# Joined attention: item order, split output products, key copies ahead of the exponential, and two moves at the end of the feed-forward stage

## The chip, the cores and the metric

The kernel runs on one core of one Trainium2 chip. The metric is the device time of one execution in microseconds (us), as a median over executions. "The profile" is one execution taken by the hardware profiler; its times are from the start of its span. Engines: PE is TensorE (PEld its weight loads), DVE is VectorE, ACT is ScalarE, POOL is GpSimd, SP is SyncE, which here only issues DMAs.

## The reference, cut to what matters

One decoder layer over a prompt (16 meta tokens and 1024 prompt tokens) and 8 sample sequences of 4 tokens with 2048 cached positions each:

```python
a = rmsnorm(hp, g_mix)
q_r, k_r, v_r, g_r, q_lat, q_pe, c_kv, k_pe = mixer_inputs(a, ...)   # one input projection
o_r, st = retention_prompt(q_r, k_r, v_r, log_gamma)
o_lat = mla_prompt(q_lat, q_pe, c_kv, k_pe)      # causal softmax, 4 heads, blocks of 128 queries
hp = hp + mixer_output(o_r, g_r, o_lat, w_uv, w_out)
hp = hp + conv_ffn(rmsnorm(hp, g_ffn), ...)      # up-projection, width-3 conv, silu gate, down-projection
# the sample rows do the same, with mla_attend over the paged cache (page_table) and their own tokens:
s = (einsum('bqhc,bkc->bhqk', q_lat, c_kv) + einsum('bqhr,bkr->bhqk', q_pe, k_pe)) * SOFTMAX_SCALE
p = softmax(where(mask, s, -inf)); out = einsum('bhqk,bkc->bqhc', p, c_kv)
```

After the final rmsnorm the outputs are y for prompt and samples, the new latents and rope keys, the retention states and the last convolution rows.

## The kernel before, in words

The stages follow one another: input projection (until about 330 us), retention and latent projections, the joined attention (442 to 695 us), output projection, feed-forward up-projection with convolution and gate (22 steps), down-projection (77 steps), final norm. Each product of two float32 operands of the large projections is three passes of split operands (high by high, high by low, low by high), so that PE is the busy engine.

**Attention** (`attention`, from L1180) interleaves two jobs. The prompt job has 36 *items* (`items`, L1184), one per pair of a query block j (0 to 8) and a head h (0 to 3). Item j covers 16 queries for j = 0 and 128 for the others, and its keys are 16 + 128 j columns, in `nb = j + 1` blocks. The sample job walks 32 cache *pages* (each page number of four sequences at once), one in each of the iterations k = 0 to 31. The last four iterations, k = 32 to 35, have no page. Pages form groups of four, called *probability blocks* B; at k = 4B+4 the scores of block B are reduced and exponentiated (`block_max` on DVE, `block_exp` on ACT), at k = 4B+5 its probabilities are turned and weighed against the latents (`fill probs`, `weigh`).

PE's program, iteration k, in this order: the scores of item k+1 (`score_part`); two fills that turn the page's latent keys (`keys` 0 and 1); the value products of item k-1 (`value_part`); a third fill that turns the page's rope keys (`keys` 2); the fills of block B (`probs`, `own`) if there is one; the fills that turn item k's probabilities, four blocks of 128 keys per fill (`turn`); the page's scores (`page_scores`); a `self` fill in k = 15 and 31; `weigh`; `close` and `head_values` for the end of a group of sequences.

A *fill* is a run of transposes into one of two PSUM banks of a ring (`ring_b`, fill n uses bank n % 2). PE may start fill n only when fill n-2 has been copied out (`wait_left`). Which engine copies is fixed: ACT takes `keys` 0 and 2 and the first and third `turn`; DVE takes `keys` 1, the second `turn`, `probs`, `own`, `self` and `close`. `page_scores` waits for all three keys copies, and in the first page of a block (k % 4 = 0) for `block_exp` of the block before, since that frees the bank of the page scores.

ACT's program, iteration k: copy `keys` 0; exponential of item k+1 (`exp_part`); `block_exp` if k % 4 = 0; copy `keys` 2; copies of the turns; the output of item k-1 to its high part (`hi_part`). DVE's: `block_max`; `take_part`; masking and row maximum of item k+1 (`max_part`); copy `keys` 1; `probs`, `own`, `block_sum`; the second turn; `close`; the low part of item k-1's output (`lo_part`, after `hi_part`); `self`; scaling of item k+1's probabilities (`scale_part`). `value_part(k)` waits for all turn copies of item k and for `lo_part(k-1)`; `weigh` waits for `lo_part(k-1)`.

Pages are loaded by SP and POOL, eight buffers deep. The four buffers of block B come free in `weigh(B)`. When the last page is weighed, SP also loads the first half of the output weights (`room.load_out`).

**The end of the feed-forward up-projection** (step n = NF-1 = 21). ACT: `second_out` twice, `split_d(0..3)` (high parts of the first four down-projection steps, two copies each, four buffers), `tap2` of the a half (waits for DVE's `add_first`), `first_out` of the g half (takes product 4 of the last step out of PSUM), `tap2` of the g half, `split_d(4)`, `silu`. DVE: `lo_a`, `lo_w` of steps 0 to 3, then `add_first`, the taps, steps 4 and on. PE: the down-projection. Its step 0 has four tiles of three products; tiles 2 and 3 write the banks that `first_out` must have emptied (`pe.wait_ge(S["ug1"], NF - 1 if m < 2 else NF)`). After steps 4 to 9 PE turns the convolution states (`state_turn`); when ACT has copied them all (`st_out`), SP stores them and then issues the loads of step 15 and on (`load_lanes`).

## Time and profile before

| | us |
|---|---|
| median of 3 runs | 1544.28 (1540.99 to 1544.93) |
| the profiled execution's own time | 1536.31 |
| its span | 1534.6 |
| PE busy | 1463.2 (95%) |
| DVE busy | 803.4 (52%) |
| ACT busy | 588.1 (38%) |
| POOL busy | 389.4 (25%) |

A row of the timeline gives start, length, engine, source line, operation, output <- inputs, shapes (stationary and moving operand for PE), a count of merged instructions, and in brackets how long the engine had been idle before it and what ended the idleness. PE instructions overlap, so that the distance between two starts tells the pace better than a length. PEclk is the clock granted to TensorE as a share of full speed: 1.00 is 2.4 GHz, 0.50 is 1.2 GHz.

### The profile page before, as it was taken

The numbers are of one execution on the slowest core, as the hardware profiler recorded it, in microseconds if no ns is written. First come the engines' busy times: TensorE is split into PE (matmuls) and PEld (weight loads), VectorE is DVE, ScalarE is ACT, GpSimd is POOL, SyncE is SP. The second block draws the span as 40 slices with busy tenths as digits, with TensorE's granted clock in tenths as the row PEclk, the third lists the DMA queues.
The fourth block names the chain that finished last, engine by engine and source line by source line (L and its number), as shares of the span: only waits on it lengthen the run. The fifth ranks groups of instructions, "written<-read, shape, count | busy, mean of one in ns | idle before, by whom it ended". The sixth has DMA issues, their size and how long they took to land. (4 is left out here: it accounts for less than half of the span.)

```text
span 1534.6 us, 27260 instructions
## 1 busy us (share of the span) xinstructions
PE 1463.2 (95%) x9933; PEld 1248.0 (81%) x9933; DVE 803.4 (52%) x1461; ACT 588.1 (38%) x1303; POOL 389.4 (25%) x520
## 2 busy tenths in 40 slices
PE   5999999999998999979999999999999999999997
PEld 5997877666876777757889999999999998787786
DVE  4512200153435555542159466666666666598877
ACT  5420111122434433332136354444544454443454
POOL 2136631040033423104002444443343431000000
PEclk9999999998989999998999999999999999999999
DMA  6521223342425423114331332233223335754764
GB/s 231 164 94 49 101 104 132 105 142 68 153 78 143 139 70 105 36 56 111 95 105 56 110 111 91 88 109 109 70 81 109 109 110 192 263 180 165 254 221 163
DMA packets 143362, 186.87 MB, mean 122 GB/s; under 512 B 22947, under 2 KB 89812, under 8 KB 143078
## 3 DMA queue, kind: packets, MB, share of 16 engines
q1 hardware_dynamic: 138462, 175.72, 35.2%
q0 software_dynamic: 4800, 9.84, 2.2%
q8 instruction: 60, 0.98, 0.3%
q14 instruction: 40, 0.33, 0.1%
HBM read 149.25 MB, written 36.19 MB: 121 GB/s over the span
## 5 line engine op out<-in xcount | busy, mean ns | idle before, releaser
L2929 PE MATMUL p_ff<-s_ff_th,s_ff_rhi 128*128 128x266 f32 x640 | 182.9, 286 | 0.6 <-ACT s_ff_u L2513 0.6
L2931 PE MATMUL p_ff<-s_ff_tl,s_ff_rhi 128*128 128x266 f32 x640 | 183.0, 286 | 0.0
L2932 PE MATMUL p_ff<-s_ff_th,s_ff_rlo 128*128 128x266 f32 x640 | 183.0, 286 | 0.0
L2929 PE MATMUL p_ff<-s_xh,s_ff_rhi 128*128 128x266 f32 x608 | 175.7, 289 | 6.5 <-DVE s_ff_rlo L2700 2.7
L2931 PE MATMUL p_ff<-s_xl,s_ff_rhi 128*128 128x266 f32 x608 | 174.2, 287 | 0.0
L2932 PE MATMUL p_ff<-s_xh,s_ff_rlo 128*128 128x266 f32 x608 | 173.9, 286 | 0.0
L118 PE MATMUL p_ip<-s_ip_hi,s_xh 128*128 128x512 f32 (+2 forms) x400 | 149.4, 374 | 3.4 <-DVE s_xl L216 3.4
L120 PE MATMUL p_ip<-s_ip_hi,s_xl 128*128 128x512 f32 (+2 forms) x400 | 148.5, 371 | 0.0
L119 PE MATMUL p_ip<-s_ip_lo,s_xh 128*128 128x512 f32 (+2 forms) x400 | 148.4, 371 | 0.0
L3034 PE MATMUL p_ff<-s_fd_wh,s_fd_ah 128*128 128x512 f32 x308 | 123.2, 400 | 7.2 <-DVE s_fd_wl L2808 4.3
L2929 PEld LDWEIGHTS p_ff<-s_xh,s_ff_rhi 128*128 128x128 f32 x608 | 114.9, 189 | 16.8 <-DVE s_ff_rlo L2700 8.8
L2929 PEld LDWEIGHTS p_ff<-s_ff_th,s_ff_rhi 128*128 128x128 f32 x640 | 120.9, 189 | 0.7 <-issue 0.7
L3036 PE MATMUL p_ff<-s_fd_wh,s_fd_al 128*128 128x512 f32 x308 | 121.3, 394 | 0.0
L3035 PE MATMUL p_ff<-s_fd_wl,s_fd_ah 128*128 128x512 f32 x308 | 121.2, 393 | 0.0
L2932 PEld LDWEIGHTS p_ff<-s_ff_th,s_ff_rlo 128*128 128x128 f32 x640 | 121.0, 189 | 0.0
L2931 PEld LDWEIGHTS p_ff<-s_ff_tl,s_ff_rhi 128*128 128x128 f32 x640 | 120.9, 189 | 0.0
L2932 PEld LDWEIGHTS p_ff<-s_xh,s_ff_rlo 128*128 128x128 f32 x608 | 115.2, 189 | 0.0
L2931 PEld LDWEIGHTS p_ff<-s_xl,s_ff_rhi 128*128 128x128 f32 x608 | 114.8, 189 | 0.0
L2700 DVE TENSOR_TENSOR s_ff_rlo<-s_ff_scr,s_ff_rhi 128x512 fp32r<-128x512 f32 x60 | 49.4, 823 | 90.4 <-ACT s_ff_rhi L2485 90.2
L118 PEld LDWEIGHTS p_ip<-s_ip_hi,s_xh 128*128 128x128 f32 x400 | 76.4, 191 | 16.4 <-DVE s_xl L216 3.8
L119 PEld LDWEIGHTS p_ip<-s_ip_lo,s_xh 128*128 128x128 f32 x400 | 76.3, 191 | 11.2
L120 PEld LDWEIGHTS p_ip<-s_ip_hi,s_xl 128*128 128x128 f32 x400 | 76.2, 191 | 11.1
(308 smaller groups left out, 3119.7 us busy)
## 6 DMA issues: line engine op xcount, KB each, us to landing
s_ff_raw<-in_w_up SPq DMA_DIRECT2D x44, 512.0 KB, 4.6
s_fd_lanes<-in_w_down SPq DMA_DIRECT2D x77, 256.0 KB, 3.3
s_fd_lanes<-a_rows SPq DMA_DIRECT2D x66, 256.0 KB, 3.5
a_rows<-s_ff_cv SPq DMA_DIRECT2D x22, 512.0 KB, 2.9
s_ff_scr<-in_w_down SPq DMA_DIRECT2D x11, 1024.0 KB, 5.8
s_pages<-in_cache_kv_latent SPq DMA_DIRECT2D x68, 128.0 KB, 2.1
s_ip_raw<-in_w_in SPq DMA_DIRECT2D x4, 2048.0 KB, 8.7
s_pages<-in_cache_kv_latent POOLq DMA_DIRECT2D x60, 128.0 KB, 2.4
```

The source lines that it names most:

```text
L118: pe.matmul(out, hi_w, hi_x, start=first, stop=False)
L119: pe.matmul(out, hi_w, lo_x, start=False, stop=False)
L120: return pe.matmul(out, lo_w, hi_x, start=False, stop=last)
L2700: dve.tensor_tensor(rlo[:, s, :], split_source(n, p), rhi[:, s, :].bitcast(F32), ALU.subtract).then_inc(S["lo"], 1)
L2929: pe.matmul(out, rhi[:, s, ks_], hi_cols(k), start=first and k == 0, stop=False, skip_group_check=True)
L2931: pe.matmul(out, rhi[:, s, ks_], lo_cols(k), start=False, stop=False, skip_group_check=True)
L2932: mm = pe.matmul(out, rlo[:, s, ks_], hi_cols(k), start=False, stop=last and k == 3, skip_group_check=True)
L3034: pe.matmul(out, ah[:, r, ts], wh[:, r, :], start=first, stop=False, skip_group_check=True)
L3035: pe.matmul(out, ah[:, r, ts], wl[:, r, :], start=False, stop=False, skip_group_check=True)
L3036: return pe.matmul(out, al[:, r, ts], wh[:, r, :], start=False, stop=last, skip_group_check=True)
```

## The change

1. The items' order of query blocks is 8, 7, 6, 5, 3, 2, 1, 0, 4 in place of 0 to 8. Two wait counts that assumed the blocks of j = 8 last are counted by `last_tiles`.
2. `value_part` becomes `value_first` (all waits and the first `nb // 2` blocks) and `value_rest` (the others, and the signal). PE does `value_first(k-1)`, the rope `keys` fill, then `value_rest(k-1)`.
3. ACT copies `keys` 2 right after `keys` 0, in front of `exp_part(k+1)` and `block_exp`.
4. The third turn of a long item (key block 8, only for j = 8) is filled after `page_scores` and after `self`.
5. In the last up-projection step ACT does `first_out(n, 1, 1)` before `split_d(3)` and before the a half's `tap2`, and DVE does `add_first(n)` before `lo_a(2)`.

```diff
-    items = [(j, h) for j in range(NT) for h in range(H)]
+    items = [(j, h) for j in (8, 7, 6, 5, 3, 2, 1, 0, 4) for h in range(H)]
...
+        def last_tiles(i):
+            return sum(j == NT - 1 for j, _ in items[:i + 1])
...
-            for m, b0 in enumerate(range(0, geometry(k)[2], 4)):
+            for m, b0 in enumerate(range(0, min(geometry(k)[2], 8), 4)):
                 add("dve" if m == 1 else "act", "turn", k, b0)
             if k < PAGES and (k + 1) % (GBLOCKS * BP) == 0:
                 add("dve", "self", k // (GBLOCKS * BP))
+            if geometry(k)[2] > 8:
+                add("act", "turn", k, 8)
...
                     if k < PAGES:
                         empty(act, place["keys", k, 0], copy)
+                        empty(act, place["keys", k, 2], copy)
                     if k + 1 < NI:
                         exp_part(k + 1)
                     if block_at(k, 0) is not None:
                         block_exp(block_at(k, 0))
-                    if k < PAGES:
-                        empty(act, place["keys", k, 2], copy)
...
-                    for b in range(nb):
+                    value_products(i, range(geometry(i)[2] // 2))
+
+                def value_rest(i):
+                    value_products(i, range(geometry(i)[2] // 2, geometry(i)[2])).then_inc(S["out_done"], 1)
...
                     if k:
-                        value_part(k - 1)
+                        value_first(k - 1)
                     if k < PAGES:
                         fill(place["keys", k, 2])
+                    if k:
+                        value_rest(k - 1)
...
-                    for n in turns(k):
+                    for n in turns(k)[:2]:
                         fill(n)
                     if k < PAGES:
                         page_scores(k)
                         if (k + 1) % (GBLOCKS * BP) == 0:
                             fill(place["self", k // (GBLOCKS * BP)])
+                    for n in turns(k)[2:]:
+                        fill(n)
...
                 second_out(n, 1, 0)
-                for i in range(4):
+                for i in range(3):
                     split_d(i)
+                first_out(n, 1, 1)
+                split_d(3)
                 tap2(n, 1, 0)
-                first_out(n, 1, 1)
                 tap2(n, 1, 1)
...
                 lo_a(1)
                 lo_w(1)
+                add_first(n)
                 lo_a(2)
                 lo_w(2)
                 lo_a(3)
                 lo_w(3)
-                add_first(n)
```

## Rows read from the trace of the kernel before

**Rows 1.** The page: busy time of an engine; granted PE clock in 40 slices.
```profile
PE 1463.2 (95%) x9933; PEld 1248.0 (81%) x9933; DVE 803.4 (52%) x1461; ACT 588.1 (38%) x1303; POOL 389.4 (25%) x520
PEclk9999999998989999998999999999999999999999
```
**Rows 2.** Busy time in the attention's stretch (PE, PEld, DVE, ACT, POOL, PEclk).
```profile
446.20:695.30 249.10, 228.08 (x2270) 172.82 (x2269) 124.56 (x356) 92.43 (x282) 64.85 (x123) 0.97 0.33 95
```
**Rows 3.** Waits of PE: sum, times, longest.
```profile
PE p_at_turn L1720 <- ACT s_da_keys L1403: 4.0, 5, 1.0
PE p_ff L3034 <- ACT s_ff_u L2499: 2.9, 1, 2.9
PE p_at_block L1730 <- ACT s_da_keys L1403: 1.8, 3, 0.7
```
**Rows 4.** Timeline of PE, iteration k = 24 (item j = 6).
```profile
591.62 1.03 PE L1689 MATMUL p_at_turn<-s_ident,s_pages 128*128 128x128 f32 x8
...
595.53 0.55 PE L1720 MATMUL p_at_turn<-s_ident,s_pa_p 128*128 128x128 f32 x3 [0.88 <-ACT s_da_keys L1403]
596.00 0.64 PE L1730 MATMUL p_at_block<-s_da_keys,s_da_qlat 128*32 128x128 f32 x16
```
**Rows 5.** Timeline of ACT, the same iteration.
```profile
593.35 0.91 ACT L1411 ACTIVATE s_pa_p<-p_at_score,s_pa_mx 128x784 f32<-128x784 f32 x1 [0.50 <-DVE s_pa_mx L1486]
...
594.91 0.29 ACT L1429 ACTIVATE s_da_sm<-s_da_mx 128x1 f32<-128x1 f32 x1
595.10 0.38 ACT L1403 ACTIVATE s_da_keys<-p_at_turn 128x256 f32<-128x256 f32 x1
```
**Rows 6.** Timeline of PE, k = 8 (item j = 2).
```profile
490.41 0.64 PE L1730 MATMUL p_at_block<-s_da_keys,s_da_qlat 128*32 128x128 f32 x16 [0.65 <-ACT s_da_keys L1403]
```
**Rows 7.** Timeline of PE and DVE, k = 31: scores of a j = 8 item end.
```profile
649.15 1.03 PE L1689 MATMUL p_at_turn<-s_ident,s_pages 128*128 128x128 f32 x8
651.29 0.69 DVE L1467 COPY s_da_keys<-p_at_turn 128x512 f32<-128x512 f32 x1
```
**Rows 8.** Timeline of PE, iterations without a page and the next stage.
```profile
663.36 0.33 PE L1720 MATMUL p_at_turn<-s_ident,s_pa_p 128*128 128x128 f32 x1 [2.64 <-ACT s_pa_pt L1403]
...
681.65 0.33 PE L1720 MATMUL p_at_turn<-s_ident,s_pa_p 128*128 128x128 f32 x1 [1.29 <-ACT s_pa_pt L1403]
...
691.00 4.18 PE L1664 MATMUL p_at_mix<-s_pa_pt,s_vt 128*128 128x128 f32 x18 [0.66 <-DVE s_xl L1570]
698.58 0.50 PE L118 MATMUL p_ff<-s_op_split,s_xh 128*128 128x512 f32 x1 [3.40 <-POOL s_op_split L2013]
```
**Rows 9.** Timeline of DVE and ACT, maximum and exponential of a j = 4 item.
```profile
533.17 0.71 DVE L1478 TENSOR_REDUCE s_pa_mx<-p_at_score 128x1 f32<-128x528 f32 x1
534.10 0.70 ACT L1411 ACTIVATE s_pa_p<-p_at_score,s_pa_mx 128x528 f32<-128x528 f32 x1 [0.36 <-DVE s_pa_mx L1486]
```
**Rows 10.** Granted clock in short stretches (PE busy, PEclk; in the second DMA).
```profile
455.00:456.00 1.00, 0.70 (x7) 0.50 0.83 207
1300.00:1302.00 2.00, 2.00 (x6) 0.50 1.05 385
```
**Rows 11.** Timelines of ACT, DVE and PE, start of the down-projection.
```profile
1294.76 0.62 ACT L2583 ACTIVATE s_fd_wh<-s_fd_kb 128x512 fp32r<-128x512 f32 x1
1298.36 0.71 ACT L2499 ACTIVATE s_ff_u<-p_ff 128x32 f32<-128x32 f32 x3
...
1296.10 0.83 DVE L2733 TENSOR_TENSOR s_ff_u<-p_ff,s_ff_u 128x32 f32<-128x32 f32 x3
...
1299.12 0.50 PE L3034 MATMUL p_ff<-s_fd_wh,s_fd_ah 128*128 128x512 f32 x1 [2.88 <-ACT s_ff_u L2499]
...
1303.07 0.43 PE L3035 MATMUL p_ff<-s_fd_wl,s_fd_ah 128*128 128x512 f32 x1
1303.34 0.39 PE L3036 MATMUL p_ff<-s_fd_wh,s_fd_al 128*128 128x512 f32 x1
```
**Rows 12.** The chain that ended last, and a PE wait of the timeline after it.
```profile
1338.11 4.42 DMA s_fd_lanes<-a_rows
...
1391.61 0.47 PE L3034 MATMUL p_ff<-s_fd_wh,s_fd_ah 128*128 128x512 f32 x1 [0.27 <-DVE s_fd_wl L2808]
```

More of the change, by code:

```diff
@@ L1277, in turns @@
         def turns(i):
-            n = place["turn", i, 0]
-            return range(n, n + (geometry(i)[2] + 3) // 4)
+            return [place["turn", i, b0] for b0 in range(0, geometry(i)[2], 4)]
         def scores(i):
@@ L1484, in max_part @@
                         dve.tensor_tensor(most, mx[0:nq, i, 0:1], mx[0:nq, i, 1:2], ALU.max).then_inc(S["max_b"], 1)
-                        dve.wait_ge(S["max_b"], i + 1 - H * (NT - 1))
+                        dve.wait_ge(S["max_b"], last_tiles(i))
                     dve.tensor_scalar(mx[0:nq, i, 3:4], most, -SCALE, None, ALU.mult).then_inc(S["max_c"], 1)
@@ L1494, in scale_part @@
                         dve.tensor_tensor(whole, sm[0:nq, i, 0:1], sm[0:nq, i, 1:2], ALU.add).then_inc(S["sum_a"], 1)
-                        dve.wait_ge(S["sum_a"], i + 1 - H * (NT - 1))
+                        dve.wait_ge(S["sum_a"], last_tiles(i))
                     dve.reciprocal(sm[0:nq, i, 3:4], whole).then_inc(S["sum_b"], 1)
@@ L1649, in score_part, with value_first @@
                     m.then_inc(S["scored"], 1)
-                def value_part(i):
-                    h, (_, nq, nb) = items[i][1], geometry(i)
+                def value_first(i):
                     for n in turns(i):
@@ L1662, in value_part, with value_products @@
                         pe.wait_ge(R["lo_out"], closed(i - 1) + 1)
-                    for b in range(nb):
+                    value_products(i, range(geometry(i)[2] // 2))
+                def value_rest(i):
+                    value_products(i, range(geometry(i)[2] // 2, geometry(i)[2])).then_inc(S["out_done"], 1)
+                def value_products(i, blocks):
+                    h, (_, nq, nb) = items[i][1], geometry(i)
+                    m = None
+                    for b in blocks:
                         m = pe.matmul(out_of(i)[:, 0:nq], vt[:, b, h * DK:(h + 1) * DK], pt[:, i % 2, b, 0:nq],
                                       start=b == 0, stop=b == nb - 1, skip_group_check=True)
-                    m.then_inc(S["out_done"], 1)
+                    return m
                 def fill(n):
@@ L1826, in _ @@
                         head_values(closed(k - 1))
-                value_part(NI - 1)
+                value_first(NI - 1)
+                value_rest(NI - 1)
 UW = DEC_B * (DEC_T + 2)
```

## The prediction

> **What bounds the kernel now.** I read the page first: PE is busy 95% of the span and no other engine above 52% [rows 1]. So a microsecond is won only where PE stands still or runs at its lower clock. The reader is to see in the clock line that PE has the full 2.4 GHz nearly everywhere. Next I read the waits of PE, then its timeline with what ended each idle time. In the attention (446.20 to 695.30 us) PE is busy 228.08 of 249.10 us, so 21.0 us are idle [rows 2]. The timeline names 18.2 us of them in 30 waits above 0.15 us. Three families matter. Eight waits are put down to ACT's copy of the rope keys, 4.0 + 1.8 = 5.8 us [rows 3]. Nine waits stand in the iterations without a page, from 2.64 us to 0.66 us, together 8.5 us [rows 8]. The other 13 are small and sum to 3.9 us. Outside the attention, the change touches one PE wait of 2.88 us at the start of the down-projection [rows 3, 11].
>
> **The key copy in front of the exponential (edits 2 and 3).** The name of the releaser says that the 5.8 us go. I don't believe it, since in seven of the eight places the waiting iteration is one with a `block_exp`, and there `page_scores` also waits for `block_exp`. Take k = 24. The scores of item 25 end at 591.62. The exponential starts at 593.35 (+1.73), `block_exp` ends with the instruction of 594.91, the key copy starts at 595.10, the turn goes at 595.53 and `page_scores` at 596.00, which is +4.38 [rows 4, 5]. Now let the copy go first. PE reaches the rope keys after the two fills (0.87 us) and half the value products. A block of value costs 0.22 us: the four blocks in front, when the item before has eight, cost 0.89. The copy is done near +0.87 + 0.89 + 0.38 (the fill) + 0.38 (the copy) = +2.5. The exponential starts there and no more at +1.73. From its start to the end of `block_exp` are 595.10 - 593.35 = 1.75 us, with the signal 1.85 to 1.95. So `page_scores` can start at +2.5 + 1.95 = +4.45, and before it was +4.38. The wait is not gone; it changes its releaser from the key copy to `block_exp`. What PE does up to that point is longer when the item before is longer, so idle time is what I count. By the same sum I get for the seven block iterations: k = 4 (j = 7) 0.15, k = 8 (j = 6) 0.55, k = 12 (j = 5) 0.55, k = 16 (j = 3) 1.1, k = 20 (j = 2) 1.05, k = 24 (j = 1) 1.05, k = 28 (j = 0) 1.25: together 5.7 us. In the short ones 0.15 to 0.85 us of it is the DVE copy of `keys` 1, which stands behind `block_max` and isn't touched. Before, the same seven iterations have 6.2 us, of which k = 8 has 0.65 for the rope keys [rows 6] and 0.42 for DVE. The gain is 0.5 us. Further, k = 31 loses its 0.56 us wait and gets 0.45 for DVE's `keys` 1 copy, and the three waits of 0.28 us in k = 1 to 3 fall to 0.1. Of the 13 small waits those of `weigh` and `own` move to other k and stay about the same (1.5 us), since the delay of up to 0.8 us that the exponential takes is covered by PE's value products and turns in long items.
>
> **The item order (edit 1).** Its total work on each engine is the same. What moves are the seams.
> - The start, k = 0. It has no value products. A j = 8 item needs 651.29 - 649.15 = 2.14 us from the end of its scores to the start of the DVE copy of `keys` 1, which takes 0.69 [rows 7]. PE needs the copy after 0.87 us of fills and 0.22 of rope keys: it waits 2.14 + 0.69 - 1.09 = 1.75, about 1.8 us. Before it was 0.26. Cost 1.5 us.
> - The end, k = 32 to 35, now has j = 4 items. I walked it instruction by instruction with the durations of the rows: scores 1.8 us, value 1.12, turns 0.75, `weigh` with `own` 2.5, maximum 1.2 with a reduction of 0.71, exponential 0.9 with its 0.70 [rows 9], `block_max` 1.45, `block_exp` 1.1, first turn copy 0.64, output parts 0.55. PE waits before value(32) 2.0 (behind `block_max`, maximum, exponential, `block_exp`, turn copy, output parts), before turn(33) 0.7, before `weigh` 1.15, before value(34) 1.3, before `head_values` 1.1, before the last value 0.65. Sum 6.9 us against 8.5 [rows 8]: gain 1.6 us. The chain got shorter, but so did PE's work that covers it.
> - The pages come at the same pace from SP and POOL (about 3.3 to 3.5 us a page at issue). After `weigh` of block 5 at k = 25, page 28 is needed three iterations later, some 8 us, and lands some 5.5 us after; page 31 has more room. Cost nothing; if that cover is too short, the price is the difference, up to 2 us at each of k = 28 and 29.
> - The output weights are asked for some 12 us before the attention ends, in place of 20. They land in about 6. Nothing.
> - The third turn behind `page_scores` (edit 4): in k = 1 to 3 the first turn's copy is done 0.4 to 0.8 us before PE comes to it. Nothing left to pay; the cover is `page_scores`, 1.06 us.
>
> Sum of the idle time in the attention: 0.3 (start) + 1.8 + 5.7 + 1.5 + 0.45 + 0.3 + 6.9 = 16.95 against 18.2, so -1.3 us. Bounds: -6 (the key waits really go) and +4 (each short iteration waits half a microsecond more).
>
> **The clock.** PE is at 0.50 from 443.0 to 456.6 us [rows 10], in which it does products of 16 and 32 columns and transposes. Behind the meta scores, at 446.2, there is now the score of a j = 8 item, 5.3 us of 512-column products at the low clock. The two low stretches in 512-column work (699.0 and 1299.7) last 3.4 us each, this one 13.7. If it lasts 3.4 us less, PE gets back half of that, 1.7 us; I take this, between 0 and 3.4. At the end of the attention the last values took 4.18 us [rows 8] where the same 18 matmuls took 2.17 at full clock, and `head_values` 2.6 where it took 1.5; I leave that cost as it is.
>
> **The end of the up-projection (edit 5).** ACT finishes `split_d(3)` with the copy at 1294.76, waits for DVE's `add_first` (1296.10, three instructions, 0.83), does the tap (1.28) and only then `first_out` (1298.36, 0.71). PE has waited from 1296.24 to 1299.12 [rows 11]. With the edit, `first_out` starts when `split_d(2)` is done, at 1294.05, since its product was complete well before, and ends at 1294.8. PE wants it at 1296.24: the 2.88 us go. `split_d(3)` and `lo_w(3)` end near 1296.9, and PE needs them after three steps of 2.73 us, at 1302.9: covered by 6 us. `add_first` (0.83) in front of `lo_a(2)` is covered likewise, step 2 being wanted at 1300.2 and ready at 1295.6. What is late next: nothing on PE before step 15. Directly behind the wait the clock falls to 0.50 [rows 10]; until 1303.07 eight matmuls take 3.4 us where the pace after is 0.23 each, 1.8 us. With no wait I expect no fall: 1.55 us more. Together 4.4.
>
> Does that reach the end? The chain that ended last passes through SP's loads of step 15 and their landing, 4.42 us [rows 12]. They are issued when the turned states are copied, and these follow PE's steps, so they move with it. From 1342.6 on DVE is busy nearly without a gap, and PE waits 0.27 us for it at 1391 [rows 12]: PE is not ahead of DVE there. So PE's gain counts in full only if the loads move as far as PE. The store of the last gated rows, on which the earlier loads wait, moves only by some 1.3 us, and the DMA engines were full there. Bounds 0 and 4.4; I take 4.4, since the store was not the last thing those loads waited for.
>
> **Sum.** -1.3 - 1.7 - 4.4 = -7.4 us. The profiled execution would go from 1536.31 to 1528.9. It lies 8.0 us below the median of the three runs; carried over to the median 1544.28, the forecast is 1536.9 us.
>
> A rule of the Trainium skill bears on the tail. In "TensorE: Matmul & The Clock Gate", section "HAM oscillation — how this bites in real kernels", waits between short bursts of products bring the low clock back again and again. This case's trace agrees in part: behind the 2.88 us wait the clock fell, behind the 2.64 us wait at 663 it did not. By the rule the time would be that of rival C below, by the rows that of the forecast.
>
> **Rivals.**
> - A, the key waits really go (chance 0.13). For it: the profile names ACT's key copy as releaser eight times [rows 3]. Against it: the walk through k = 24. Then 5.3 us more are won in the block iterations: 1531.6.
> - B, the down-projection takes its gain back (0.22). PE arrives 4.4 us earlier at the stretch where DVE and the loads set the pace, and waits there. For it: 0.27 us waits on DVE at 1391, and DMA engines full. Against it: the loads follow PE. What is left is attention and clock, -3.0: 1541.3.
> - C, slower (0.08): short items at the end leave PE with less cover, and the low clock takes the whole of k = 32 to 35. PE's work there is 18 us; at half clock it costs 18 more, less the 3.1 us that were paid before, and 1.7 in the next stage: +16.6. With -7.4 that gives 1553.5. It decides from 15 us of additional low clock on, since each of them costs half a microsecond. For it: PE idle a quarter of that stretch, and the fall at 688.7. Against it: before, the stretch from 655 to 688 was idle for nearly as large a part at full clock. The named section of the skill speaks for this rival.
> - D, the pages come late at k = 28 and 29 (0.05): +4, which gives 1540.9.
>
> **Chances.** The forecast has 0.52. What this kernel's measurement can tell from no change is about 0.3%, 4.6 us. Faster: 0.85 of the forecast's share, all of A, a quarter of B, a third of D: 0.64. Slower: C, 0.08. Within: 0.28. The range is 1530 to 1544: below it is A with more clock than I gave it, above it C and a part of B with the start paying more than 1.8 us.
>
> **What would show it.** Right: PE's waits on `s_da_keys` L1403 nearly gone in block iterations, with waits of `p_at_block` on ACT's `s_da_p` or `s_da_sm` (the `block_exp` lines) in their place, each about half a microsecond to one; a wait of 1.8 us at the first page's turn; six waits in the last four iterations with some 7 us in sum; no wait of L3034 on `s_ff_u` and no low clock behind it. Wrong: attention shorter by over 4 us of idle; PE waiting on DVE's `s_fd_wl` for 3 us more than the 4.3 us in total of before; a low clock from k = 32 on; a PE wait on the page loads.

## The result, and the profile after

| | before | changed |
|---|---|---|
| median | 1542.63 us (1538.57 to 1544.93, 4 runs) | 1526.34 us (1521.87 to 1530.38, 4 runs) |
| ratio | | 0.9896, 95% interval 0.986 to 0.9933 |
| span of the profiled execution | 1534.6 | 1525.8 |
| its granted clock, mean | 0.981 | 0.984 |

The forecast was 1536.9 us, range 1530 to 1544. The kernel is faster by 16.3 us, and the gain forecast was 7.4. The two profiled spans are only 8.8 us apart: the profiled execution of before was a fast one, as more runs show below.

The page after has as busy a PE as [rows 1], for 8.6 us less:

```profile
PE 1454.6 (95%) x9933; PEld 1244.1 (82%) x9933; DVE 799.0 (52%) x1461; ACT 585.2 (38%) x1303; POOL 390.5 (26%) x520
PEclk9999999998989999998999999999999999999999
```

By stage (first score of the attention; first matmul of the output projection; first of the up-projection; first of the down-projection; end), before and after: attention 256.1 and 250.4 us, output projection 114.5 and 114.9, up-projection 481.6 and 484.1, down-projection 240.0 and 234.9. The gain lies where the edits are, in the attention and the down-projection. (No edit touches the body of the up-projection. The 481.6 is the shortest of all 17 profiles of this document; the other 16 have 483.0 to 485.3.)

The waits of PE after, attention and down-projection (sum in us, times, longest), against [rows 3]:

```profile
PE p_ff L3050 <- DVE s_fd_wl L2824: 4.4, 9, 2.0
...
PE p_at_mix L1674 <- DVE s_xl L1507: 2.7, 2, 1.9
PE p_at_turn L1730 <- DVE s_da_p L1470: 2.4, 5, 0.7
PE p_at_turn L1730 <- DVE s_da_keys L1470: 2.3, 4, 1.1
...
PE p_at_block L1740 <- ACT s_da_sm L1433: 1.3, 2, 0.7
PE p_at_turn L1704 <- ACT s_da_keys L1407: 1.3, 4, 0.3
...
PE p_at_block L1740 <- ACT s_da_p L1438: 0.8, 1, 0.8
...
PE p_at_block L1740 <- ACT s_da_p L1429: 0.5, 2, 0.2
```

The turns and the page scores hardly wait for ACT's rope-key copy any more (5.8 us before, one wait of 0.3 now); the page scores wait for `block_exp` (lines 1429 to 1438) in its place, and `s_ff_u` has gone from the down-projection. The idle time that the timeline names in the attention was 18.2 us between its first score and the first projection matmul, and is 18.7 now. By that view the attention should have gained nothing. It became 5.7 us shorter, and its clock loss is nearly the same in these two profiles (10.2 and 9.8 us, the time at half clock taken half).

The waits of the last four iterations in PE's timeline, answering to [rows 8] (rows without a wait between them are left out):

```profile
666.27 1.35 PE L1674 MATMUL p_at_mix<-s_pa_pt,s_vt 128*128 128x128 f32 x10 [1.92 <-DVE s_xl L1507]
668.85 0.73 PE L1730 MATMUL p_at_turn<-s_ident,s_pa_p 128*48 128x128 f32 x5 [0.68 <-DVE s_da_p L1470]
670.73 0.63 PE L1770 MATMUL p_at_mix<-s_da_own_b,s_da_p 4*32 4x256 f32 x8 [1.16 <-DVE s_pa_pt L1470]
677.77 0.44 PE L1721 MATMUL p_at_turn<-s_ident,s_da_ol 128*128 128x128 f32 x2 [0.91 <-ACT s_pa_pt L1407]
679.01 2.36 PE L1674 MATMUL p_at_mix<-s_pa_pt,s_vt 128*128 128x128 f32 x10 [0.81 <-DVE s_xl L1507]
683.53 1.93 PE L1789 MATMUL p_at_mix<-s_da_olf,s_w_uv 128*128 128x16 f32 x16 [1.10 <-DVE s_xl L1507]
686.12 2.47 PE L1674 MATMUL p_at_mix<-s_pa_pt,s_vt 128*128 128x128 f32 x10 [0.66 <-DVE s_xl L1573]
```

Together 7.2 us, where 6.9 were forecast. The start of the down-projection in ACT, DVE and PE, answering to [rows 11]:

```profile
1290.60 0.61 ACT L2598 ACTIVATE s_fd_wh<-s_fd_kb 128x512 fp32r<-128x512 f32 x1
1290.62 0.83 DVE L2749 TENSOR_TENSOR s_ff_u<-p_ff,s_ff_u 128x32 f32<-128x32 f32 x3
...
1290.93 0.39 PE L3050 MATMUL p_ff<-s_fd_wh,s_fd_ah 128*128 128x512 f32 x1
1291.13 0.74 ACT L2514 ACTIVATE s_ff_u<-p_ff 128x32 f32<-128x32 f32 x3
```

`first_out` begins 0.20 us behind PE's first matmul of the stage and is over at 1291.87, 0.45 us before the third tile, the first that needs it (1292.32). PE doesn't stop.

### The profile page after: what moved, and what is told of

It reads as the page before. It is cut to its first block and busy times, and to the rows that moved or that the text cites. A ratio compares the mean times of both kernels' runs of the same rounds, so it can differ in the third digit from the quotient of the medians.

```text
span 1525.8 us, 27257 instructions
## 1 busy us (share of the span) xinstructions
PE 1454.6 (95%) x9933; PEld 1244.1 (82%) x9933; DVE 799.0 (52%) x1461; ACT 585.2 (38%) x1303; POOL 390.5 (26%) x520
```

## The experiments

They were timed in four sessions, in each of which the kernel before ran too: base_again, down_only, split_only and copy_only (mean of before 1541.8 us); order_only, long_first, tail_four and no_order (1541.2); after_again, extra_scores, after_long and late_block_exp (1542.7); split_copy, copy_turn and turn_only (1541.1). One program's mean thus moves by up to 1.6 us between sessions, so a second reading of the same executions is used, which removes part of the scatter. Each lists its span and its mean granted clock c. **Clock loss** is (1 - c) x span; **rest** is the time less that. It is a rough split, since low clock costs nothing where PE waits anyway. What stands behind +- is half of a 95% interval. Over 109 executions of the kernel before, the mean time is 1541.6 us, the clock loss 31.8 and the rest 1509.7 (+- 0.35), and time and loss go together with a correlation of 0.94; their standard deviation falls from 4.1 us (time) to 1.9 (rest): most of what scatters is the clock. Eight executions far apart from the others are left out (seven that took over 1600 us and, in the means of base_again, one whose mean clock of 0.929 doesn't fit its time).

| kernel | edits | median us | ratio, 95% interval | mean us | clock loss | rest |
|---|---|---|---|---|---|---|
| before, 109 executions | none | 1540.98 to 1542.95 | | 1541.6 | 31.8 +- 0.9 | 1509.7 +- 0.4 |
| base_again | none | 1542.42 | 1.0001, 0.9972 to 1.003 | 1542.2 | 33.3 +- 1.1 | 1508.8 +- 0.7 |
| down_only | 5 | 1537.18 | 0.9967, 0.9937 to 0.9997 | 1536.7 | 29.5 +- 2.4 | 1507.2 +- 1.1 |
| split_only | 2 | 1541.48 | 0.9988, 0.9956 to 1.002 | 1540.1 | 30.9 +- 2.6 | 1509.1 +- 1.4 |
| copy_only | 3 | 1547.39 | 1.0028, 0.9997 to 1.006 | 1547.8 | 34.6 +- 2.6 | 1513.2 +- 0.7 |
| turn_only | 4 | 1542.89 | 1.0007, 0.9985 to 1.0028 | 1542.2 | 33.3 +- 2.2 | 1509.0 +- 0.9 |
| copy_turn | 3, 4 | 1549.59 | 1.0065, 1.0044 to 1.0085 | 1550.1 | 37.2 +- 1.9 | 1512.9 +- 0.9 |
| split_copy | 2, 3 | 1536.28 | 0.9969, 0.9951 to 0.9987 | 1536.4 | 29.2 +- 1.9 | 1507.2 +- 0.6 |
| no_order | 2 to 5 | 1532.82 | 0.995, 0.9933 to 0.9967 | 1533.1 | 29.5 +- 2.9 | 1503.6 +- 0.8 |
| order_only | 1 | 1537.02 | 0.9984, 0.9968 to 1.0001 | 1537.4 | 29.7 +- 3.0 | 1507.7 +- 1.5 |
| long_first | order 8, 0, 1 ... 7 | 1533.27 | 0.9956, 0.9932 to 0.998 | 1533.9 | 24.0 +- 2.1 | 1509.9 +- 0.9 |
| tail_four | order 0 to 3, 5 to 8, 4 | 1538.59 | 0.999, 0.997 to 1.001 | 1539.2 | 31.9 +- 3.1 | 1507.3 +- 0.9 |
| after_again | all | 1528.22 | 0.9911, 0.9888 to 0.9933 | 1528.0 | 26.2 +- 1.8 | 1501.8 +- 1.8 |
| after_long | all, order 8, 0 ... 7 | 1529.11 | 0.9901, 0.9874 to 0.9927 | 1528.8 | 26.6 +- 5.0 | 1502.2 +- 1.2 |
| extra_scores | none, 1024 columns more | 1544.53 | 1.0018, 0.9993 to 1.0043 | 1545.1 | 30.2 +- 3.3 | 1514.9 +- 1.0 |
| late_block_exp | all, one move more | 1523.93 | 0.988, 0.9852 to 0.9907 | 1523.9 | 23.3 +- 3.5 | 1500.6 +- 1.1 |

The ten executions of the changed kernel (the four of the result, six of after_again) have a mean of 1527.3, a clock loss of 25.3 and a rest of 1501.9.

**base_again**: no edit, to see what a comparison of equals gives.

> The kernel before, once more: it tells how far one profile and five timed runs of the same program spread. If the profiled execution of before was a lucky one (1536.31 against a median of 1542.63), this profile lies nearer to 1542; if profiling itself is faster than timing, it lies again some 6 us below. No change from before: ratio 1.000 within 0.3%.

Its span was 1538.4 at clock 0.979, where the profiled execution of before had 1534.6 at 0.981. The named idle time of the attention was 18.2 us in both. So the profile behind the prediction was representative in its waits and not in its clock.

**down_only**, edit 5:

```diff
-                for i in range(4):
+                for i in range(3):
                     split_d(i)
+                first_out(n, 1, 1)
+                split_d(3)
                 tap2(n, 1, 0)
-                first_out(n, 1, 1)
...
+                add_first(n)
                 lo_a(2)
                 lo_w(2)
                 lo_a(3)
                 lo_w(3)
-                add_first(n)
```

> Before plus edit 5 alone (first_out before split_d(3), add_first before lo_a(2)). Theory: the 2.88 us wait and the low clock behind it go and the gain reaches the end whole: -4.4 to -5.0 us. Rival: the gain is taken back where DVE and the loads set the pace: -0 to -2 us, and PE's waits on s_fd_wl grow.

The mean fell by 5.1 us. The stage went from 240.0 us to 235.6, with no low clock at its start. Of the eleven profiles that keep the old order of this stage, nine show low clock there, for 3.4 or 6.8 us, and none of the six with edit 5 does. The length of the wait alone doesn't decide it: it was 2.7 to 4.2 us in the nine, and in order_only it was 3.35, with the clock at 1.00 for the next 10 us:

```profile
1300.26 0.50 PE L3037 MATMUL p_ff<-s_fd_wh,s_fd_ah 128*128 128x512 f32 x1 [3.35 <-ACT s_ff_u L2502]
```

That PE arrives early and waits for DVE, rival B, is refuted by the length of the stage and by the sum of its waits on DVE behind 1285 us, 4.3 us before and 4.5 now:

```profile
PE p_ff L3035 <- DVE s_fd_wl L2809: 4.5, 10, 2.0
```

**split_only**, edit 2:

```diff
-                        value_part(k - 1)
+                        value_first(k - 1)
                     if k < PAGES:
                         fill(place["keys", k, 2])
+                    if k:
+                        value_rest(k - 1)
...
```

> Before plus edit 2 alone (half the value products behind the rope keys' fill, ACT's order as before). Theory H, a wait that no idle time shows: in every page iteration the second turn waits about 0.26 us for ACT's copy of the rope keys, since only one turn fill lies between; with half a value product in between it goes: -4 to -6 us, and no gain in the listed idle time. Rival N, only listed idle time counts: within 1 us of before.

**copy_only**, edit 3:

```diff
                         empty(act, place["keys", k, 0], copy)
+                        empty(act, place["keys", k, 2], copy)
                     if k + 1 < NI:
                         exp_part(k + 1)
...
-                    if k < PAGES:
-                        empty(act, place["keys", k, 2], copy)
```

> Before plus edit 3 alone (ACT copies keys 2 ahead of the exponential; PE's order as before). Theory H: the rope keys are filled behind the whole value product, so the exponential and block_exp come 0.5 to 1.3 us later in each page iteration; the listed waits on ACT's key copy go, waits on block_exp take their place: +2 to -2 us. Rival, the releaser's name is right: the 5.8 us of listed waits go: -5 to -6 us.

Both expectations missed. By the means of their session the halved products alone give 1.7 us, where 4 to 6 were expected and which is too little to tell from nothing; the copy alone costs 6, where 2 either way were expected (3.7 of the 6 are rest, 2.5 clock loss). PE's waits of copy_only show why the copy costs:

```profile
PE p_at_block L1729 <- ACT s_da_sm L1429: 4.1, 4, 1.3
PE p_at_block L1729 <- ACT s_da_p L1425: 1.9, 2, 1.1
...
PE p_at_block L1729 <- ACT s_da_p L1434: 1.6, 1, 1.6
```

The 5.8 us on the rope keys have become 7.6 on `block_exp`. The exponential now stands behind a copy that PE makes possible only after all value products.

**order_only**, edit 1; **long_first** and **tail_four**, one end of it each:

```diff
-    items = [(j, h) for j in range(NT) for h in range(H)]
+    items = [(j, h) for j in (8, 7, 6, 5, 3, 2, 1, 0, 4) for h in range(H)]   # order_only
+    items = [(j, h) for j in (8, 0, 1, 2, 3, 4, 5, 6, 7) for h in range(H)]   # long_first
+    items = [(j, h) for j in (0, 1, 2, 3, 5, 6, 7, 8, 4) for h in range(H)]   # tail_four
```

> Before plus edit 1 alone (items 8, 7, 6, 5, 3, 2, 1, 0, 4). Theory C, the clock: the profiles so far show the low clock from about 441 us on for 13.7, 13.7 and 20.5 us in three copies with the attention's order of before, and for 10.2 us in the changed kernel, and the j = 8 scores in front are what ends it: 4 to 10 us faster than before, with 10 us or less at low clock from 441 on. Rival T, only the last four iterations and the waits named there matter (8.5 to 6.9 us, and 1.5 us more at the start): within 2 us of before.

> Before with the items 8, 0, 1, 2, 3, 4, 5, 6, 7: only the four long ones come first, and the last four iterations have j = 7. Theory C: as fast as order_only within 2 us at the start, since the start is the same up to the fourth item; low clock from 441 on for 10 us or less, 4 to 8 us faster than before. If the short items behind the long ones bring the low clock back, it shows as a second stretch near 485 us. Rival T: no faster than before.

> Before with the items 0, 1, 2, 3, 5, 6, 7, 8, 4: short ones first as before, only the last four iterations are the changed kernel's. Theory C: the low clock from 441 on stays at 13 us or more, and the time within 2 us of before (1.6 us less waiting at the end). Rival T: all of the order's gain is here, 4 us or more.

The two ends act on different terms. A long item first leaves the rest where it was (1509.9) and takes the clock loss from 31.6 (before, timed beside it) to 24.0. Middle items last leave the clock loss (31.9) and take the rest down by 2.3 us. order_only's clock loss, 29.7, has an interval that reaches both; its mean is 3.8 us below before, between what theory C and rival T gave it. long_first (7.3 us) fits theory C, and tail_four (2.0) refutes rival T. The clock of the first 36 us of the attention (the last three columns are PEclk, DMA share, GB/s), of the kernel before, copy_only, order_only, long_first and after_again:

```profile
442.45:478.45 36.00, 32.55 (x331) 25.48 (x331) 14.44 (x62) 12.83 (x45) 18.66 (x40) 0.81 0.55 153
```
```profile
442.44:478.44 36.00, 33.25 (x227) 26.57 (x227) 11.30 (x50) 10.24 (x36) 18.71 (x40) 0.53 0.54 152
```
```profile
442.14:478.14 36.00, 33.08 (x206) 23.19 (x207) 15.43 (x46) 11.77 (x29) 18.95 (x40) 0.86 0.55 152
```
```profile
438.61:474.61 36.00, 32.71 (x240) 23.45 (x240) 16.43 (x49) 13.90 (x37) 19.57 (x40) 0.95 0.54 152
```
```profile
439.06:475.06 36.00, 34.03 (x248) 24.72 (x249) 17.41 (x51) 14.02 (x37) 18.84 (x40) 0.95 0.55 152
```

In the ten profiles that start with the shortest items (before, base_again, down_only, turn_only, tail_four, split_only, split_copy, copy_turn, no_order, copy_only) the clock is 0.81, 0.72, 0.81, 0.76, 0.81, 0.86, 0.86, 0.76, 0.67 and 0.53, mean 0.76. In the six that start with j = 8 (order_only, long_first, the profile after, after_again, after_long, late_block_exp) it is 0.86, 0.95, 0.86, 0.95, 0.81 and 0.91, mean 0.89. That is 0.13 x 36 = 4.7 us of clock loss, and 3.8 without copy_only, the lowest.

**no_order**, edits 2 to 5 in the old order; **after_again**, the changed kernel in another session:

```diff
-    items = [(j, h) for j in (8, 7, 6, 5, 3, 2, 1, 0, 4) for h in range(H)]
+    items = [(j, h) for j in range(NT) for h in range(H)]
```

> Edits 2 to 5 without the order of the items. Theory C with H (the hidden wait for the rope keys, about 0.25 us an iteration, which the split of the value products takes away): split -2 to -4, key copy now free of charge 0 to -2, down-projection -5: 7 to 11 us faster than before, and 5 to 8 us slower than the changed kernel. Rival, the order is worth nothing: as fast as the changed kernel (16 us).

> The changed kernel once more, beside the same runs of before as the next three. The parts measured alone are -2.5 us (order) and -7.7 us (edits 2 to 5), sum -10. If they simply add up: 9 to 11 us faster than before. If the order is worth more with the other edits, because their short iterations lengthen the low clock at the start when the order is the old one: 14 to 17 us, as first measured.

Against down_only, no_order has the same clock loss and a rest 3.6 us lower: edits 2, 3 and 4 together give what neither 2 nor 3 gives alone. after_again is 14.8 us faster than before by the means of its session, more than the 10 that the parts measured until then add up to, so that the edits are worth more together.

**extra_scores**, the kernel before with the scores of one more j = 8 item (1024 columns, unused) at the start:

```diff
+                q = slice(col0(NT - 1), col0(NT - 1) + P)
+                for half in range(2):
+                    score(score_b[:, 2 + half, :], 0, q, slice(T0 + 512 * half, T0 + 512 * half + 512))
```

> Before, and ahead of the first item's scores PE computes 1024 columns of scores of a j = 8 item into two PSUM banks that nobody reads: 6 matmul groups of 512 columns, pure extra work of 2.7 us at full clock, 5.3 at low. Theory C: these dense products end the low clock early, as the long items do: low clock from 441 on for 10 us or less, and the time no more than 1 us above before, or below it. Rival, the order matters for something else than the clock: the low stretch stays at 13 us or more and the kernel is 4 to 5 us slower.

In its profile the clock of the first 36 us was 0.95, and the page fills of k = 8 came 44.5 us behind the attention's start, where the profile of before had 44.7 without the extra work. But over twelve executions the clock loss fell by only 3.0 +- 4 against before in the same session, and the rest rose by 5.4, twice what the expectation gives for the extra products at full clock; why twice isn't known. The runs don't settle whether long columns at the start alone shorten the low clock; they show that this added work doesn't pay.

**after_long**, the changed kernel in the order 8, 0, 1 ... 7, that is with long items last:

```diff
-    items = [(j, h) for j in (8, 7, 6, 5, 3, 2, 1, 0, 4) for h in range(H)]
+    items = [(j, h) for j in (8, 0, 1, 2, 3, 4, 5, 6, 7) for h in range(H)]
```

> The changed kernel with the items 8, 0, 1, ..., 7: the long ones first, then the old order, j = 7 at the end. If only the first four items matter for the start and the end is indifferent: within 2 us of the changed kernel. If j = 4 at the end is worth something: 2 us or more slower. If short items in the middle hurt less than at k = 16 to 31: up to 3 us faster.

It can't be told from the changed kernel, in time or in either part. But its mean has an interval of 4 us, so that this run excludes no effect of the tail as small as that of tail_four.

**late_block_exp**, the changed kernel with the last `block_exp`, k = 32, behind the turn copies and the output part on ACT:

```diff
-                    if block_at(k, 0) is not None:
+                    if block_at(k, 0) is not None and k < PAGES:
                         block_exp(block_at(k, 0))
...
+                    if block_at(k, 0) is not None and k >= PAGES:
+                        block_exp(block_at(k, 0))
```

> The changed kernel, with ACT doing block_exp of the last block (k = 32) behind the turn copy and the output's high part instead of in front. The wait of 1.92 us before value(32) should fall to about 0.9, and the one before turn(33) should stay near 0.7: 1 to 2 us faster than the changed kernel, too small for the times alone, visible in the waits. Rival: the last probabilities' turn is then late by as much, nothing won.

PE's wait in front of the value products of item 32 fell from 1.92 us to 0.80, and the other six stayed:

```profile
661.42 1.35 PE L1676 MATMUL p_at_mix<-s_pa_pt,s_vt 128*128 128x128 f32 x10 [0.80 <-DVE s_xl L1509]
```

It has the lowest median of all. Its rest is 1.2 us below after_again's, what the wait gave, but within their intervals.

**split_copy**, **copy_turn** and **turn_only** ask which pair makes the 3.6 us; their edits are the pieces of the diff by their numbers. The last one's is

```diff
-                    for n in turns(k):
+                    for n in turns(k)[:2]:
                         fill(n)
...
+                    for n in turns(k)[2:]:
+                        fill(n)
...
```

> Edits 2 and 3 without 4 (old item order, old start of the down-projection). Theory P (pairing: the halved output products give PE something to do while ACT copies the rope keys, and the copy ahead takes away the short waits in each iteration; the third turn has no part in it): the time apart from the low clock falls by some 3.6 us, to about 1506, and the ratio to the kernel before is near 0.998; the second fill of the turns starts 0.75 us after the first where it is 1.0 to 1.1 in the kernel before. Rival T (the third turn's place makes the gain): no gain here, 1509 or more, ratio 1.000 to 1.003.

> Edits 3 and 4 without the halved output products. Theory P: it stays slower, since nothing stands between the rope keys' fill and the turns that could be done ahead of the copy: rest about 1513, ratio 1.002 to 1.004, as the key copy alone. Rival T: the rest falls to about 1506, ratio below 0.999.

> Edit 4 alone: the third turn of the four j = 8 items behind the page's scores. In the old order three of these items stand where there is no page, so that only k = 32 could change. Theory P: nothing, rest 1509 to 1510, ratio 0.999 to 1.001. Rival T: a gain of over 1 us.

The pair is the halved products and the copy: 4.7 us by the means of the session, 3.0 in the rest. The copy without them is slower again, with or without the third turn, whose place changes nothing in the old order. There it can move only k = 32. In the new order it acts in k = 1 to 3, and no run takes it out alone; from order_only to the changed kernel these three iterations became 0.73, 0.73 and 0.56 us shorter, and which part of that is edit 4's stays open. The clearest measure is the stretch from the page fills of k = 8 to those of k = 31, the same work in all kernels of the old order. Before, split_only, copy_only and split_copy, in turn (length, PE busy; PEclk is 1.00 in each):

```profile
487.10:649.15 162.05, 153.83 (x1571) 115.06 (x1570) 83.83 (x221) 63.92 (x181) 43.38 (x80) 1.00 0.32 90
```
```profile
485.47:646.14 160.67, 152.52 (x1571) 115.89 (x1570) 83.94 (x221) 62.69 (x181) 43.36 (x80) 1.00 0.32 91
```
```profile
494.42:659.65 165.23, 153.70 (x1572) 115.18 (x1571) 84.72 (x221) 60.94 (x181) 43.53 (x80) 1.00 0.31 88
```
```profile
485.74:645.39 159.65, 151.17 (x1571) 116.13 (x1570) 84.63 (x221) 61.73 (x181) 43.16 (x80) 1.00 0.32 91
```

So -1.4 for the halves, +3.2 for the copy, -2.4 for both, which is 4.2 less than the two added up. no_order has -2.3 (159.71 us), and down_only, whose attention is that of before, 162.07: at full clock the stretch repeats to 0.1 us. (In base_again, turn_only, extra_scores and copy_turn it holds 3.4 us of low clock and can't be compared; base_again has 163.48.) And the reader is to see that in split_copy PE is *busy* 2.7 us less for the same 1571 matmuls at the same clock. Its busy time had held waits.

## Why the prediction was wrong

Against the mean of the many executions of before, the changed kernel gives 14.3 us: edit 5 gives 5.1 (down_only), edits 2 to 4 give 3.6 (no_order less down_only), and edit 1 gives 5.8 (the changed kernel less no_order). The forecast had 4.4, 1.1 and 1.8. (Sessions differ by up to 1.6 us, and so the split isn't sharper than that. In the other sequence order_only gives edit 1 3.8, and leaves 5 for edits 2 to 4 in the new order.) So two terms of the sum failed: the waits in the page iterations, of which the walk priced only what PE's rows name, and the clock at the start. The other 3.7 us of the 10.6 between forecast and median aren't the change's: the median that the forecast started from was 2.7 above that mean, and the median of the changed kernel's four runs lies 1.0 below its mean over ten.

**The end of the up-projection: right.** Mechanism and size held: 4.4 us were forecast and the stage of down_only is 4.4 shorter. The wait of 2.88 us and the low clock behind it [rows 10, 11] went, step 3 wasn't late, and the gain reached the end. The cover was thinner than forecast: `first_out` is over 0.45 us before PE wants its banks, where the forecast times leave 1.4.

**The waits of the block iterations: right in what replaces what, wrong in the sum.** The idle time that the walk gave the seven block iterations came as forecast, 5.5 us for 5.7 (0.25, 0.65, 0.66, 0.83, 0.93, 0.93 and 1.23 from k = 4 to 28). The small waits around it grew where the walk left them: 2.9 us at the probabilities, `own`, `weigh` and the first `head_values` for 1.5, and 1.3 in k = 29 to 31 behind the key copies for 0.45. So the attention has 18.7 us of named idle time where the sum had 16.95, and became shorter all the same. The step that failed is the one that says "The gain is 0.5 us" and counts only idle time that the timeline names. In the stretch above, that idle rose from 6.7 to 8.0 us with edits 2 and 3, and the stretch became 2.4 shorter: 3.7 us of waiting went that no PE row names. Most of it is in the iterations without a block, which the walk left out but for k = 1 to 3 and 31. Here is k = 23 (item j = 5) before, PE, its weight loads and ACT:

```profile
587.55 1.07 PE L1720 MATMUL p_at_turn<-s_ident,s_pa_p 128*48 128x128 f32 x6
587.75 0.38 ACT L1403 ACTIVATE s_da_keys<-p_at_turn 128x256 f32<-128x256 f32 x1
588.19 0.20 PEld L1720 LDWEIGHTS p_at_turn<-s_ident,s_pa_p 128*128 128x128 f32 x2 [0.27 <-ACT s_da_keys L1403]
588.55 0.64 PE L1730 MATMUL p_at_block<-s_da_keys,s_da_qlat 128*32 128x128 f32 x16
```

and with edits 2 and 3 (split_copy):

```profile
584.93 0.38 ACT L1403 ACTIVATE s_da_keys<-p_at_turn 128x256 f32<-128x256 f32 x1 [0.73 <-PE p_at_turn L1700]
585.33 0.65 PEld L1726 LDWEIGHTS p_at_turn<-s_ident,s_pa_p 128*48 128x48 f32 x6
585.39 0.82 PE L1726 MATMUL p_at_turn<-s_ident,s_pa_p 128*48 128x128 f32 x6
586.14 0.64 PE L1736 MATMUL p_at_block<-s_da_keys,s_da_qlat 128*32 128x128 f32 x16
```

The same six transposes take 1.00 us to the next start before, and 0.75 after. PE's row shows no wait in either: its matmuls carry lengths that overlap, and a stop of a quarter of a microsecond vanishes under them. The second turn fill uses the bank of the rope keys, and the weight load of its first transpose waits for ACT's copy. In copy_only the same iteration goes like this:

```profile
597.06 1.07 PE L1719 MATMUL p_at_turn<-s_ident,s_pa_p 128*48 128x128 f32 x6
597.26 0.38 ACT L1403 ACTIVATE s_da_keys<-p_at_turn 128x256 f32<-128x256 f32 x1 [1.40 <-PE p_at_turn L1693]
...
597.70 0.20 PEld L1719 LDWEIGHTS p_at_turn<-s_ident,s_pa_p 128*128 128x128 f32 x2 [0.27 <-ACT s_da_keys L1403]
```

ACT stands ready and copies at once, but only the first turn fill lies between the rope fill and the second, and the wait stays 0.27. In split_only the copy is behind the exponential and the wait is again 0.27 at k = 23. The view that would have shown this ahead is the waits of the weight loads. For k = 8 to 31, before, split_only and copy_only (split_copy has no such row):

```profile
PEld p_at_turn L1720 <- ACT s_da_keys L1403: 7.3, 15, 1.2
```
```profile
PEld p_at_turn L1727 <- ACT s_da_keys L1403: 5.1, 7, 1.2
```
```profile
PEld p_at_turn L1719 <- ACT s_da_keys L1403: 3.5, 13, 0.3
```

In that stretch of before the weight loads wait 15 times on the rope-key copy: four times long, in the block iterations, and eleven times for 0.23 to 0.28 us, which PE's rows don't name. PE's rows name 3.4 of the 7.3 us, and the other 3.9 are close to the 3.7 that went. (With edit 2 the rope-key fill itself waits for ACT five times for 0.22 us, where before it did once, so that the match is not exact.) Edit 2 alone takes away eight of the eleven short ones and none of the long ones; edit 3 alone turns the long ones into waits on `block_exp` and leaves the short ones. Only both together leave none. And what the copy alone costs, 3.2 us in this stretch, is all named idle time (6.7 us before, 10.0 in copy_only). "Perfetto Trace Analysis" of the Trainium skill, section "Tensor Engine Instruction (MATMUL, LD_WEIGHTS)", says that the end of a PE instruction in a profile is estimated and not observed. The rows fit that, with 1.00 and 0.75 us to the next start under rows of 1.07 and 0.82, but no run here shows how the ends come about.

**The clock at the start: the term was mis-sized, and so was its base.** The step took 1.7 us, between 0 and 3.4, for a low stretch of 13.7 us that becomes 10.3. The stretch of before was one draw. In the three other profiles that leave the attention as it was or change only the third turn it was 20.5 us, 13.7 and 17.1, and the first 36 us lost 4.7 us more clock than with a long item first (mean of ten profiles and of six). Edit 1 shows 4.2 us of its 5.8 in clock loss (29.5 to 25.3), and long_first 7.6. Each of these has an interval of some 3 us. Nor is all of it at the start for certain: order_only and long_first are the two profiles whose clock didn't fall at the old down-projection. Why the low clock lasts longer under the short items stays argued: extra_scores put the same long columns in front of them, and didn't give the loss back beyond doubt.

**The start's wait and the tail: right.** The first page's turn waits 1.15 us for `keys` 1, and 0.25 more go to the rope fill, 1.4 in all where 1.8 were forecast:

```profile
459.29 0.44 PE L1704 MATMUL p_at_turn<-s_ident,s_pages 128*128 128x128 f32 x2 [0.25 <-ACT s_da_keys L1407]
460.88 1.06 PE L1730 MATMUL p_at_turn<-s_ident,s_pa_p 128*48 128x128 f32 x8 [1.15 <-DVE s_da_keys L1470]
```

The last iterations' waits are within 0.1 us of the walk, but for the one before value(34) (1.7 in two pieces for 1.3). tail_four measures the gain as 2.3 +- 1.2 us where 1.6 were expected. What is left of edit 1, a rest lower by 1.6 us where the walk has 0.1, is hardly larger than its own interval of 1.4 and stays open.

**The rivals.** A (the key waits go for good) is refuted by copy_only and by the `s_da_sm` and `s_da_p` waits of the profile after; that the time fell to its figure and below has other causes. B by down_only. C, a low clock through the whole tail, didn't come at its price: from 679.1 on there are 13.7 us at the low clock, where the profile of before had 10.2 in its tail, the least of all. It came closer than one profile shows. In after_again PE was at the low clock without a break from 673.9 to 691.0 us, through the last 10 us of the attention and into the output projection:

```profile
673.90:690.90 17.00, 11.90 (x46) 10.43 (x45) 5.40 (x7) 5.59 (x13) 4.87 (x5) 0.50 0.33 61
```

The five profiles that end with j = 4 have 13.7 to 20.5 us of low clock in stretches that begin between 655 and 715 us, at the end of the attention or just behind it, mean 17.7, and the ten of the old order 10.2 to 23.9, mean 16.0. So the tail at the low clock was there before, and the change adds some 2 us to it and not the 15 from which on C decides. The Trainium skill, "TensorE: Matmul & The Clock Gate", section "HAM oscillation — how this bites in real kernels", was taken in the prediction as speaking for C. These tails agree with it in part: low clock comes back among waits of 0.7 to 1.9 us, but in the old order as much, and the time is not that of C. D would show as PE waits on page loads, of which the profile after has none.

## What to carry to other kernels

Where matmuls overlap, read the waits of the weight loads and the distances between starts beside PE's named idle time; a stop of 0.27 us that recurs in most iterations is worth as much as the rows with a large number. A copy moved ahead on its engine gains only if the matrix engine has work between what feeds the copy and what waits for it; moved alone it delays what stood in front of it (here +3.2 us in the stretch alone, -2.4 with the cover). And before a low-clock stretch of one profile is priced, look at it in several executions: it was the part that scattered most, and the order of the work around it seems to have moved it by 4 us, more than any wait of the attention that this change took away.

## What the runs showed of the hardware

Most of the scatter of this kernel's time goes with the granted clock. With each execution's loss at the low clock taken away, the standard deviation over 109 executions of before falls from 4.1 to 1.9 us, and an effect like the 2.3 +- 1.2 us of tail_four stands out that its ratio leaves unclear. split_only's doesn't, even so.

In all 17 profiles PE waits 2.05 us in front of the attention's first matmul, and the clock falls to 1.2 GHz between 0.1 us ahead of that matmul and 3.2 us behind it, though PE is then busy (12.84 of the 13.60 us at the low clock in the profile of before). This low clock lasted 10.2 to 34.1 us in the ten profiles that begin with the same short items, the longest in copy_only, where the first 36 us had a clock of 0.53, and 3.4 to 13.7 in the six that begin with j = 8. At the old start of the down-projection a wait of 2.7 us went with low clock (copy_turn), and one of 3.35 did not (order_only). What decides isn't shown by these runs.
